# Expert gate/up products split over the depth, and modulation slices summed on VectorE, in a transformer block on one Trainium2 core

## What is computed

```python
c_act = jax.nn.silu(c)
mod = (c_act @ w_ada[l] + b_ada[l])[:, None, :]          # 1024 x 6144 weights
shift1, scale1, gate1, shift2, scale2, gate2 = jnp.split(mod, 6, axis=-1)
...
merged = jax.nn.sigmoid(zg_conv) * y_conv + jax.nn.sigmoid(zg_mla) * y_mla
x = x + gate1 * (merged @ w_o[l])
h2 = rms_norm(x, norm2_g[l]) * (1.0 + scale2) + shift2
...
for g in range(N_GROUPS):
    a = jax.nn.silu(jnp.einsum('bsd,edf->bsef', h, w_gate[g])) * jnp.einsum('bsd,edf->bsef', h, w_up[g])
    a = a * comb[:, :, g, :, None]
    out = out + jnp.einsum('bsef,efd->bsd', a, w_down[g])
x = x + gate2 * out
```

## Time and profile before

| what | us |
|---|---|
| median of 3 runs | 537.07 |
| lowest, highest run | 534.3, 537.37 |
| the profiled execution | 534.07 |
| its span, first to last instruction | 532.2 |

### The profile page before, as it was taken

How to read it: one execution, slowest core, us unless ns; L and a number is a source line. 1 busy time by engine, 2 the same in 40 slices (tenths; PEclk the granted TensorE clock), 3 DMA queues, 4 the chain that set the end, 5 groups by cost and what they waited for, 6 DMA issues and landing times.

```text
span 532.2 us, 14859 instructions
## 1 busy us (share of the span) xinstructions
PE 497.3 (93%) x6205; PEld 388.0 (73%) x6206; DVE 183.7 (35%) x559; ACT 148.1 (28%) x276; POOL 153.0 (29%) x195
## 2 busy tenths in 40 slices
PE   4799999999999999999999969998999899899994
PEld 3687888888888888888888746665666566566663
DVE  0631624242424252424231442332233223233333
ACT  3012222223232222313131242323322332233221
POOL 0000010101010101010100015767676676677672
PEclk9899999999999999999999999999999999999999
DMA  8997317394959563624446974979999999999982
GB/s 352 418 442 291 139 60 283 119 426 177 437 203 431 195 248 152 249 121 159 158 159 238 389 323 180 369 308 427 427 435 429 434 425 432 432 427 434 422 342 80
DMA packets 10689, 161.94 MB, mean 304 GB/s; under 512 B 1184, under 2 KB 2464, under 8 KB 3104
## 3 DMA queue, kind: packets, MB, share of 16 engines
q1 hardware_dynamic: 10656, 161.45, 73.7%
HBM read 160.40 MB, written 1.05 MB: 303 GB/s over the span
## 4 chain that ended last, share of the span: by engine, by line
PE 85%; DMA 10%; issue 2%; DVE 1%; ACT 1%; SPq 0%; DVEq 0%; ACTq 0%
PE ps L476 81%; DMA wex<-in_ex 7%; DMA wex<-in_ada 3%; PE ps L744 1%; PE ps L770 1%; PE ps L745 1%; DVE xT L1068 1%; ACT act L449 0%; ACT L452 0%; PE ps L649 0%; PE ps L662 0%; PE ps L663 0%; PE ps L664 0%; SPq L285 0%; ACT work L452 0%
## 5 line engine op out<-in xcount | busy, mean ns | idle before, releaser
L476 PE MATMUL ps<-act,wmix 128*128 128x256 f32 x864 | 194.1, 381 | 1.0 <-DVE act L850 1.0
L476 PEld LDWEIGHTS ps<-act,wmix 128*128 128x128 f32 x864 | 161.6, 190 | 24.6 <-issue 3.5
L357 POOL TENSOR_SCALAR work<-trig,work 128x256 f32<-128x256 f32 x70 | 64.9, 936 | 61.9 <-issue 52.6
L476 PE MATMUL ps<-wex,work 128*32 128x128 f32 (+1 forms) x1840 | 70.5, 300 | 11.0 <-issue 9.8
L343 POOL TENSOR_TENSOR work<-work,trig 64x256 f32<-64x256 f32 x8 | 5.7, 718 | 252.9 <-ACT work L410 151.2
L476 PE MATMUL ps<-work 32*128 32x256 f32 (+6 forms) x864 | 72.7, 374 | 0.6 <-ACT work L470 0.6
L476 PEld LDWEIGHTS ps<-wex,work 128*32 128x32 f32 x1840 | 50.1, 111 | 28.5 <-issue 13.7
L476 PEld LDWEIGHTS ps<-work 32*128 32x128 f32 (+3 forms) x864 | 47.5, 168 | 13.3 <-issue 3.3
L467 ACT ACT_TABLE_LOAD x35 | 44.9, 1283 | 1.0 <-issue 0.4
L476 PE MATMUL ps<-act,work 128*32 128x256 f32 (+1 forms) x704 | 42.6, 362 | 2.5 <-DVE work L1035 1.3
L361 POOL TENSOR_TENSOR work<-work,trig 128x512 f32<-128x512 f32 x35 | 44.6, 1275 | 0.0
(11 more groups left out here) (181 smaller groups left out, 421.8 us busy)
## 6 DMA issues: line engine op xcount, KB each, us to landing
wex<-in_ex SPq DMA_DIRECT2D x20, 3072.0 KB, 18.5
wex<-in_ada SPq DMA_DIRECT2D x12, 2048.0 KB, 11.3
wmix<-in_ex SPq DMA_DIRECT2D x8, 3072.0 KB, 20.5
wmix<-in_mix_even SPq DMA_DIRECT2D x4, 3200.0 KB, 10.5
wmix<-in_mix_odd SPq DMA_DIRECT2D x4, 3008.0 KB, 10.7
work<-in_ex SPq DMA_DIRECT2D x4, 2048.0 KB, 19.8
wmix<-in_wo SPq DMA_DIRECT2D x2, 2048.0 KB, 8.0
act<-in_ex SPq DMA_DIRECT2D x4, 1024.0 KB, 16.7
```

What stands on the lines that cost most here:

```text
L357: nc.gpsimd.tensor_scalar(comb_both[:, rows], slot_row[:, rows], lane_now, None, ALU.is_equal).then_inc(comb_half, 1)
L476: return nc.tensor.matmul(out, lhsT, rhs, start=start, stop=stop, **kw)
```

## The change

1. **Gate/up split over the depth.** Column group q now takes the depth tiles 2q and 2q + 1 and all 512 columns: 8 products of 32x512 instead of 32 of 32x128. Each group of 32 partitions holds a part of the sum. VectorE copies all 512 columns. Four products with 128 columns of that copy as weights and a new constant `stack` (four identity matrices of 32, one above another) as the moving side add the four parts and transpose them at once; they stand in place of one transpose. The turned rows go to bank 3 instead of bank 0, which the wider result fills.
2. **The heads' slices summed by VectorE.** `ada_steps` multiplies the 8 depth tiles of a slice by the conditioning vector, one scalar per partition, and adds them up into `ada_sum` (512 columns) in 8 steps, 5 after `conv_gated` and 3 in the middle of the head. TensorE then sums over the partitions: 4 products with `ones` as weights instead of 32.
3. **The transfer.** The next slice is asked for when VectorE has summed the one before, and ahead of the next head's weights in SyncE's order.

```diff
@@ -294,20 +296,23 @@
             def beside_load(j):
-                sp.wait_ge(ada_done, 4 + j)
+                if j == 0:
+                    sp.wait_ge(ada_done, 4)
+                else:
+                    sp.wait_ge(ada_summed, j)
                 sp.dma_start(ada_beside, ada_d[4 + j]).then_inc(ada_landed[3], 16)
...
             for c in range(HEADS):
+                if c + 1 < HEADS:
+                    beside_load(c + 1)
                 if c + 2 < HEADS:
                     mix_load(c + 2)
                 else:
                     ring(WO0 + c + 2 - HEADS, wo_d[c + 2 - HEADS])
                 if 1 <= c < OWN:
                     expert_load(c - 1, c - 1)
-                if c + 1 < HEADS:
-                    beside_load(c + 1)
@@ -639,8 +644,10 @@
-                pe.wait_ge(ada_landed[3], 16 * h + 32)
-                ada_item(ada_beside, ps[:, 0, 0:P]).then_inc(ada_done, 1)
+                pe.wait_ge(ada_summed, h + 1)
+                for q in range(4):
+                    last = mm(ps[q * WIN:(q + 1) * WIN, 0, 0:P], ones[:, 0:WIN], ada_sum[:, q * P:(q + 1) * P], True, True)
+                last.then_inc(ada_done, 1)
@@ -741,8 +748,8 @@
-                nc.tensor.transpose(ps[:, 0, P:2 * P], rows_sb[:, 0:P], ident)
-                nc.tensor.transpose(ps[:, 0, 2 * P:3 * P], rows_sb[:, P:T], ident).then_inc(rows_turned, 1)
+                nc.tensor.transpose(ps[:, 3, T:T + P], rows_sb[:, 0:P], ident)
+                nc.tensor.transpose(ps[:, 3, T + P:2 * T], rows_sb[:, P:T], ident).then_inc(rows_turned, 1)
@@ -760,14 +767,16 @@
-                for k in range(KT):
+                for i in range(2):
                     for q in range(4):
-                        last = mm(ps[q * WIN:(q + 1) * WIN, 0, 0:P], xw[:, k, :], place_gu(place, k)[:, q * P:(q + 1) * P], k == 0, k == KT - 1)
+                        last = mm(ps[q * WIN:(q + 1) * WIN, 0, :], xw[:, 2 * q + i, :], place_gu(place, 2 * q + i), i == 0, i == 1)
                 last.then_inc(gu_ready, 1)
                 gather(n + 1)
 
                 pe.wait_ge(gu_copied, n + 1)
-                nc.tensor.transpose(ps[:, 1, 0:P], gu_sb, ident).then_inc(gu_turned, 1)
+                for c in range(4):
+                    last = mm(ps[:, 1, c * WIN:(c + 1) * WIN], gu_sb[:, c * P:(c + 1) * P], co("stack"), True, True)
+                last.then_inc(gu_turned, 1)
                 combine(n)
@@ -900,8 +909,23 @@
+            def ada_steps(j, steps):
+
+                w = ada_beside.rearrange("p (k c) -> p k c", k=KT)
+                if steps[0] == 0:
+                    dve.wait_ge(ada_landed[3], 16 * j + 32)
+                    dve.wait_ge(ada_done, 4 + j)
+                for k in steps:
+                    if k == 0:
+                        link(v.tensor_scalar(ada_sum, w[:, k, :], c_rep[:, k, 0:1], None, ALU.mult))
+                    elif k < KT - 1:
+                        link(v.scalar_tensor_tensor(ada_sum, w[:, k, :], c_rep[:, k, 0:1], ada_sum, ALU.mult, ALU.add))
+                    else:
+                        v.scalar_tensor_tensor(ada_sum, w[:, k, :], c_rep[:, k, 0:1], ada_sum, ALU.mult, ALU.add).then_inc(ada_summed, 1)
+
             conv_taps(0)
             conv_gated(0)
+            ada_steps(0, range(0, 5))
@@ -915,9 +939,12 @@
                 if h % 2 == 0:
                     dve.wait_ge(qx_ready, h // 2 + 1)
                     link(v.tensor_tensor(q_r, q_x, cos_t, ALU.mult))
+                    ada_steps(h, range(5, KT))
                     dve.wait_ge(swap_ready, h // 2 + 1)
...
+                if h % 2 == 1:
+                    ada_steps(h, range(5, KT))
                 dve.wait_ge(rk_sqrt, h + 1)
@@ -954,6 +981,7 @@
                 if h + 1 < HEADS:
                     conv_gated(h + 1)
+                    ada_steps(h + 1, range(0, 5))
@@ -1050,7 +1078,7 @@
                 dve.wait_ge(gu_ready, n + 1)
-                v.tensor_copy(gu_sb, ps[:, 0, 0:P]).then_inc(gu_copied, 1)
+                v.tensor_copy(gu_sb, ps[:, 0, :]).then_inc(gu_copied, 1)
```

More of the change, by code:

```diff
@@ L36 @@
 CONST_WIDTHS = (("ident", P), ("before", P), ("swap", P), ("slot_no", WIN), ("lane_no", 1), ("mask", T),
-                ("group_no", GROUPS), ("expert_no", EXPERTS), ("less_magic", EXPERTS), ("fold", 37), ("inv_freq", 1), ("row_no", 1))
+                ("stack", WIN), ("group_no", GROUPS), ("expert_no", EXPERTS), ("less_magic", EXPERTS), ("fold", 37), ("inv_freq", 1), ("row_no", 1))
 def places(widths):
@@ L145, in block_kernel @@
         xw = piece(KT * WIN).rearrange("p (k n) -> p k n", k=KT)
-        gu_sb = piece(P)
         silu_t = piece(2 * WIN)
@@ L154, in block_kernel @@
         wins = piece(2 * EXPERTS + 1)
+        gu_sb = work[:, work_at[0]:work_at[0] + 2 * FF]
         lg = piece(72).rearrange("p (t n) -> p t n", t=TT)
@@ L183, in block_kernel @@
         ada_rows = wex[:, OWN - 1, GU_COLS:GU_COLS + P]
+        ada_sum = wex[:, OWN - 1, GU_COLS + P:GU_COLS + P + ADA_TILES * P]
         def sm(name, i=0, n=None, parts=P):
@@ L228, in block_kernel @@
         ada_copied, ada_turned = sem("ada_copied"), sem("ada_turned")
+        ada_summed = sem("ada_summed")
         mod_ready = sem("mod_ready")
@@ L1041, in _ @@
             dve.wait_ge(sel_pair, 2)
-            xw_ps = ps[:, 0, P:3 * P].rearrange("p (h q n) -> p q h n", h=2, q=4)
+            xw_ps = ps[:, 3, T:2 * T].rearrange("p (h q n) -> p q h n", h=2, q=4)
             shift2 = mod[:, 24:32].rearrange("p (q h) -> p q h", h=2).unsqueeze(3).broadcast_to([P, 4, 2, WIN])
@@ L1093, in constants @@
     put("mask", mask)
+    put("stack", np.concatenate([np.eye(WIN, dtype=np.float32)] * 4))
     put("group_no", np.broadcast_to(np.arange(GROUPS, dtype=np.float32) - 100, (P, GROUPS)))
```

## The result

| | kernel before | changed kernel |
|---|---|---|
| median of the runs | 535.68 us (4 runs) | 547.61 us (4 runs, 545.87 to 548.49) |
| profiled execution | 534.07 us | 545.87 us |
| its span | 532.2 us | 544.0 us |

The ratio is 1.0233, 95% interval 1.0201 to 1.0266: slower by 2.3%, 12 us. The forecast was 544.0 us, with a range of 532 to 552. Against the median that it started from (537.07) that is 7 us slower; the measured difference is 12.

The account below looks back on a forecast made before the run. TensorE was taken to bound the kernel, with transfers just on time at the end. From the profiled 534.07 us: heads -12.2, windows +21.7, idle wait -1.0 gave 542.6; 1.4 added for the median made 544.0 us, range 532 to 552.

Parts of the forecast that it names:

- Heads, -12.2 us: Modulation slice on TensorE: 0.35 us per head instead of 1.88, saving 1.53 us in each of 8 heads.
- The gaps of VectorE: VectorE's idle stretches in the heads were to hold the added summing steps, with 1.4 us left at the tightest.
- rival C: Heads give nothing back: VectorE's steps or the slice delay the score products 1.5 us per head; 555 us; 7%.
- Gate/up product, 0: Expert window: 16 instructions for 64, same moving columns, so still 1.76 us; ends -0.05 and +0.2 us.
- Rival A: Gate/up product costs 27.5 ns per instruction whatever its columns, so 0.44 us; 517 us in all; 6%.
- The 81 and 131 ns: Skill's times for products of 128 and 512 columns with own weights; the prediction set this rule aside for the trace.
- Copy, 0.03 us: VectorE's 512-column copy in each window takes 0.69 us, nearly hidden by the gather; 0.03 us a window added.
- Fold, +0.59 us a window: Four folding products, 8 instructions at 0.106 us, take 0.85 us in place of one transpose of 0.26 us.
- Rival B: The fold costs only what a small product alone costs, 0.22 us, window change near 0; 522 us; 7%.
- The idle 0.98 us for a transfer goes away: TensorE's wait for a late expert load near the end was to vanish with longer windows: -1.0 us.
- some 16 us: Forecast margin between the last expert load's landing and its window: landings move about 3.7 us, the last window 21.
- My 1.4 us: Added to the sum of 542.6 us because the profiled execution lies at the low end of the runs.

Follow-up runs that it names:

- fold1: The changed kernel with only one of the four folding products, the other three quarters of the gate/up result left out; 522.63 us, one execution.
- experts_only: Only the experts' part (8 wide products, wide copy, four folding products) on the kernel before, heads as before; 560.26 us, ratio 1.0475.
- after_fill: The changed kernel with 32 small products (128 instructions) added at TensorE's start; 550.02 us, ratio 1.027 against the kernel before.

## Why the prediction was right, and where it was off

**Heads, -12.2 us: right.** 0.36 us per head measured, 0.35 forecast; the windows begin 11.7 us sooner. The gaps of VectorE held; the tightest has 1.3 us left, 1.4 was forecast. That VectorE and the transfers cost nothing was right too, but the runs show how much hung on it: 14 us with the slice behind the weights, 20 with the late request too. The prediction put this at nothing and gave rival C 7%; it never put a price on the earlier request as such.

**Gate/up product, 0: right.** 1.74 us for 1.76. The time goes with the columns. Rival A, which went by the number of instructions, fell. The 81 and 131 ns that the prediction took from the Trainium skill, TensorE: Matmul & The Clock Gate, section Back-to-back issue gap, would give 0.7 us; the trace has 1.74.

**Copy, 0.03 us: right.** 0.69 us, and the fold starts 0.05 us after its end.

**Fold, +0.59 us a window: mis-sized.** It measured +0.75. The step that failed is "8 x 0.106 = 0.85 us, so +0.59": the 0.106 is the spacing within a row of equal products, but the 0.26 of the transpose that I took off is the whole time to the next piece, with the turn-over in it. fold1 shows that a part of 0.12 us stands beside the time per instruction. 8 x 0.112 + 0.12 = 1.02, where 1.01 was measured. That the part is the turn-over to the next piece fits the traces but was not shown by itself. Over 35 windows the 0.16 us are 5.6 us. Rival B fell with it.

**"The idle 0.98 us for a transfer goes away": wrong.** It is still there in the changed kernel:

```profile
502.70 1.07 PE L481 MATMUL ps<-work 128*32 128x256 f32 x16
...
504.74 1.92 PE L481 MATMUL ps<-wex,work 128*32 128x512 f32 x16 [0.98 <-issue]
```

At the same place of the program, the first window after the round loop, TensorE idles 0.98 us and now nothing is waited for. The profile before named a DMA, since that landed last, at 496.1 (issued at 460.9, landed 35.2 later). The same idle time without a late transfer, here and in experts_only, says that it passes at the jump out of the loop anyway. The last load now lands at 484.4 + 25.1 = 509.5 and its window comes some 20 us later. The prediction had some 16 us for this; its own terms give 0.2 + 21 - 3.7 = 17.5.

**The rest.** -12.2 + 35 x 0.74 = +13.7, and +11.8 was measured between the profiles. Most of the difference is in the first window. Its gate/up product, before and after:

```profile
318.24 3.17 PE L476 MATMUL ps<-wex,work 128*32 128x128 f32 x60 [2.59 <-issue]
```

```profile
306.50 1.92 PE L481 MATMUL ps<-wex,work 128*32 128x512 f32 x16 [2.60 <-issue]
```

Before, it ran largely at the lower clock (granted 0.59 from 318.24 to 320.00 us, 0.50 from there to 321.4), and this window took 1.67 us more to its transpose than the one of the earlier trace rows (4.41 for 2.74). After, it ran at full clock (1.00 from 306.50 to 309.23). 13.7 - 1.7 = 12.0. This differs between profiles (after_fill has 2.91 us there), as do the clocks and times between runs: the four runs of the changed kernel have granted clocks of 0.994, 0.987, 0.991 and 0.990 and 545.87, 548.49, 547.69 and 547.53 us. My 1.4 us for "the profile lies at the low end" had this sign.

**What the prediction did not see.** It treated the two parts as independent, and the sum bore it out. But the kernel before sat on a good place of its round loop by chance. The heads' part alone takes away 896 instructions, moves the loop and costs 36 us; only because the experts' part makes the loop short (some 1200 instructions, no packet in rounds 2 to 4) does the change come out at +12. That the sum of the two parts held was luck in this respect: nothing in the prediction dealt with the fetching of code. The Trainium skill, Runtime: NRT & Kernel Launch, section Instruction fetch mechanics, gives TensorE a memory of 2048 instructions and says that a taken branch stalls for a fetch when its target isn't in the current window of two pages. The runs agree with that kind of stall (51 and 55 packets for 24 and 27, 7 to 8 us at a jump back). They don't agree with a window of two pages: the kernel before jumped back over some 1740 instructions three times, fetched nothing, and stood still for 1.4 us. They also show that a loop of 1740 instructions can be kept or lost by its place; by what rule stays open.

## What to carry to other kernels

Price a piece by the distance from its start to the start of the next one, and for a replacement take spacing times count plus the turn-over that the old piece had too. Before a part of a change is dropped or kept by itself, look at the packets of the instruction queue: here a long loop on TensorE lost 46 to 47 us by code that was added or removed in front of it, and 32 small products in idle time put it back. How many it takes has to be tried, since half as many in another kernel made it worse. Here the version to keep is heads_fill: the heads' part, the old gate/up product and 32 small products at the start, 2.2% faster than before (1.9 to 2.5%).

## What was unexpected in the hardware

- Half a block of code (128 instructions) in front of a loop of some 1740 instructions: 55 instruction packets instead of 27, and 57 us, 47 of them without the padding's own time. A quarter of a block: 36 packets and some 20 us, with the long stall in one round of three. A loop of some 1200 instructions did not mind half a block.
- A semaphore increment on TensorE's queue took about 0.15 us, 128 of them nearly 20 us; 128 instructions of small products took 3.6 us.
- An idle time that the profile puts down to a DMA can be there without it: 0.98 us at the end of the round loop with and without the late transfer.
